# A decoder layer with fp32r matmuls: the memory plan is shifted by 32 bytes so that the matmul operands begin at multiples of 64

## The reference

```
h = rms_norm(x, g_mix_pre)
z = h @ w_in                                   # 1024 -> 2048
y_a = pool_mixer(z[..., :256], ...)            # trailing means of 2, 4, 8, 16 rows, a 64x64 map per head
y_b = conformer_conv(z[..., 256:768], ...)     # gate, 31-tap depthwise convolution, layer norm, silu
y_c = chunk_spatial_gating(z[..., 768:1280], ...)
y_d = short_gated_conv(z[..., 1280:], ...)     # 3 taps
o = concat([y_a, y_b, y_c, y_d]) @ w_out       # 1024 -> 1024
x = x + rms_norm(o, g_mix_post)
f = rms_norm(x, g_ffn_pre)
f = square(relu(f @ w_up)) @ w_down            # 1024 -> 4096 -> 1024
x = x + rms_norm(f, g_ffn_post)
```

## The kernel before

| tile | bytes | begins at | mod 64 |
|---|---|---|---|
| raw, w_hi, w_lo | 16,384 each | 16,512; 32,896; 49,280 | 0 |
| act_hi (line 136) | 17,408 | 77,152 | 32 |
| act_lo | 17,408 | 94,560 | 32 |
| warm; xms, xroot, xinv (lines 139 to 143) | 4; 16 each, so 32 each | 111,968; 112,000 to 112,095 | |
| p1: c_gate, h_raw, b_raw, c_short, ch_ext | | 112,608 and on | 32 |
| p1: a_ext, win, pool_d, gpre, sig, p_raw, g_ext, x0, conv, sqcv, v_raw, v_n and the rest | | 133,120 and on | 0 |
| p2: o_sb, mixc, x_in, g_mix, f_sb | | 112,608 and on | 32 |
| p2: u_hi, u_lo | 17,408 each | 169,952; 187,360 | 32 |

## Time and profile before

### The profile page before, as it was taken

The page is one execution under the profiler, slowest core; times in us unless marked ns, Lnnn a source line. Parts: engine busy times, 40 slices in busy tenths (PEclk is TensorE's granted clock), DMA queues, the critical chain, the costliest instruction groups (busy, mean ns, idle before and its releaser), DMA issues.

```text
span 2278.0 us, 33025 instructions
## 1 busy us (share of the span) xinstructions
PE 2169.0 (95%) x14425; PEld 1964.6 (86%) x14425; DVE 1083.2 (48%) x1400; ACT 755.1 (33%) x1157; POOL 115.7 (5%) x205
## 2 busy tenths in 40 slices
PE   6999999994999999999999999999999989999996
PEld 5887778784798898989899898989889989999995
DVE  3687786866523334553333346433334553324343
ACT  4423232234232223443322344332324442313141
POOL 2010111110000000000000000000000000000000
PEclk9999999996899999999999999999999999999998
DMA  7754555553132224444222244532223433222221
GB/s 245 270 203 166 206 168 204 195 182 111 58 112 93 93 93 130 139 149 138 93 93 93 93 130 161 170 95 93 93 93 114 140 124 120 86 75 93 75 75 61
DMA packets 186084, 291.88 MB, mean 128 GB/s; under 512 B 6127, under 2 KB 162452, under 8 KB 177732
## 3 DMA queue, kind: packets, MB, share of 16 engines
q1 hardware_dynamic: 160244, 167.76, 22.9%
q0 software_dynamic: 24656, 120.96, 15.1%
q10 hardware_dynamic: 1040, 1.05, 0.1%
HBM read 247.24 MB, written 42.80 MB: 127 GB/s over the span
## 4 chain that ended last, share of the span: by engine, by line
PE 68%; issue 19%; DVE 6%; ACT 4%; DMA 3%; POOL 0%; POOLq 0%; ACTq 0%; DVEq 0%
PE mm L1748 22%; PE mm L1749 22%; PE mm L1750 22%; ACT w_hi L666 2%; DVE w_lo L1111 2%; DMA mixc<-mixT_scratch 1%; DMA x_in<-in_x_prompt 1%; PE tr L1753 1%; DVE conv L1155 1%; DMA raw<-in_w_in 1%; PE tr L1977 0%; PE mm L1808 0%; DVE o_sb L1450 0%; PE tr L1774 0%; DVE conv_s L1659 0%
## 5 line engine op out<-in xcount | busy, mean ns | idle before, releaser
L1111 DVE TENSOR_TENSOR w_lo<-raw,w_hi 128x2048 fp32r<-128x2048 f32 x152 | 348.5, 2292 | 711.6 <-ACT w_hi L666 711.5
L1748 PE MATMUL mm<-act_hi,w_hi 128*128 128x512 f32 (+1 forms) x1728 | 641.4, 371 | 11.5 <-DVE act_lo L1468 6.2
L1749 PE MATMUL mm<-act_lo,w_hi 128*128 128x512 f32 (+1 forms) x1728 | 635.2, 368 | 0.0
L1750 PE MATMUL mm<-act_hi,w_lo 128*128 128x512 f32 (+1 forms) x1728 | 632.3, 366 | 0.0
L1748 PE MATMUL mm<-w_hi,u_hi 128*128 128x256 f32 (+1 forms) x2176 | 609.3, 280 | 0.8
L1750 PE MATMUL mm<-w_hi,u_lo 128*128 128x256 f32 (+1 forms) x2176 | 608.6, 280 | 0.0
L1749 PE MATMUL mm<-w_lo,u_hi 128*128 128x256 f32 (+1 forms) x2176 | 607.5, 279 | 0.0
L666 ACT ACTIVATE w_hi<-raw 128x2048 fp32r<-128x2048 f32 x152 | 291.0, 1915 | 594.7 <-PE mm L1750 589.0
L1748 PEld LDWEIGHTS mm<-w_hi,u_hi 128*128 128x128 f32 (+1 forms) x2176 | 399.5, 184 | 4.8 <-DVE u_lo L1484 3.0
L1750 PEld LDWEIGHTS mm<-w_hi,u_lo 128*128 128x128 f32 (+1 forms) x2176 | 399.6, 184 | 1.2
L1749 PEld LDWEIGHTS mm<-w_lo,u_hi 128*128 128x128 f32 (+1 forms) x2176 | 397.6, 183 | 1.6
(11 more groups left out here) (243 smaller groups left out, 1350.9 us busy)
## 6 DMA issues: line engine op xcount, KB each, us to landing
raw<-in_w_ffn_up SPq DMA_DIRECT2D x64, 1024.0 KB, 5.4
raw<-in_w_ffn_down SPq DMA_DIRECT2D x64, 1024.0 KB, 5.1
w_hi<-whi_scratch POOLq DMA_DIRECT2D x24, 1024.0 KB, 5.2
w_lo<-wlo_scratch POOLq DMA_DIRECT2D x24, 1024.0 KB, 8.0
raw<-in_w_out SPq DMA_DIRECT2D x16, 1024.0 KB, 5.2
whi_scratch<-w_hi POOLq DMA_DIRECT2D x8, 1024.0 KB, 8.3
wlo_scratch<-w_lo POOLq DMA_DIRECT2D x8, 1024.0 KB, 10.7
mixc<-mixT_scratch POOLq DMA_DIRECT2D x16, 512.0 KB, 5.9
```

The lines of the kernel that those rows point to most:

```text
L1111: DVE.tensor_tensor(w_lo[:, s, :, :], raw[:, s, :, :], w_hi[:, s, :, :].bitcast(fp32), ALU.subtract)\
L1748: PE.matmul(out, whi, xhi, start=(k == 0), stop=False)
L1749: PE.matmul(out, whi, xlo, start=False, stop=False)
L1750: return PE.matmul(out, wlo, xhi, start=False, stop=(k == K - 1))
```

## The change

`warm` is allocated before `act_hi` and no longer behind `act_lo`: `act_hi` and `act_lo` begin 32 bytes later, at 77,184 and 94,592. The three tiles `xms`, `xroot` and `xinv`, which took 96 bytes, become three parts of one tile `x_stats` of 48 bytes, rounded up to 64: every tile behind it, those of p1 and of p2 with `u_hi` and `u_lo` among them, begins 32 bytes earlier, `u_hi` at 169,920 and `u_lo` at 187,328. The four begin at multiples of 64. No instruction, wait or semaphore is added or removed, and all that uses the three names reads and writes the same elements as before.

```diff
         junk = sb("junk", [P, D], bf16)
         junk_o = sb("junk_o", [P, PC], bf16)
         junk_y = sb("junk_y", [P, PC], bf16)
+        warm = sb("warm", [P, 1])
+
 
         act_hi = sb("act_hi", [P, K, NX], f32r)
         act_lo = sb("act_lo", [P, K, NX], f32r)
 
-        warm = sb("warm", [P, 1])
-
-        xms = sb("xms", [P, NCH])
-        xroot = sb("xroot", [P, NCH])
-        xinv = sb("xinv", [P, NCH])
+
+        x_stats = sb("x_stats", [P, 3, NCH])
+        xms, xroot, xinv = (x_stats[:, i, :] for i in range(3))
         sms = sb("sms", [NS, 3])
         oms = sb("oms", [P, NCH + 1, NP])
         osum = sb("osum", [P, NCH + 1])
```

## The result

The changed kernel takes 2255.09 us (median of 4 runs, 2253.35 to 2255.92) against 2274.12 for the kernel before (its three runs and one more): ratio 0.9912, 95% interval 0.9897 to 0.9928. That is 19 us less, where 9 were forecast. The order of the work is the same; the busy line of the page answers to the earlier trace rows, with matmuls 28.8 and weight loads 22.3 us less busy and the other engines within 1.2 us of before.

What follows compares the result with a forecast made beforehand. The prediction took TensorE's matmul pitch as the bound; 9.3 us less from the moving operand, with all other terms zero, took the profiled 2279.85 us to 2270.6 and the median to 2265 us, with an 8-in-10 range of 2190 to 2290.

Steps and rivals of the forecast that it cites:

- What bounds the kernel: Whole kernel: TensorE's own pace, matmuls busy 2169.0 of 2278.0 us; memory places matter through matmul pitch or few waits.
- the small operations and transfers: ScalarE, VectorE, DMA, x_stats and warm: zero cost, with bounds of 2 ns an instruction and 0.5 us on few loads.
- The stationary operand: 8,736 matmuls of 256 columns, act or u stationary: zero effect taken, with 87 us of gain as one end.
- Both say zero, which I take: Stationary operand: transposes at 273 against 272 ns and 32-column loads with the 128-column pitch, read as zero effect.
- if D moves as much as U: Sign of a wrong mechanism: D stretches were to stay at 11.20 and 45.18 us while U stretches fell.
- The moving operand: 5,184 matmuls of 512 and 272 columns with act moving: 1.8 ns less each once aligned to 64, 9.3 us.
- The addresses: act and u start 32 bytes past multiples of 64, weights on multiples; the change puts all on multiples of 64.
- the likeliest case: Only the moving operand's alignment gains: 2265 us, own range 2255 to 2271, chance 0.35.
- Whole pieces: Rival: reader fetches 64-byte pieces, alignment saves one per matmul; 2237 us, or 2190 with the stationary operand; chance 0.22.
- No change: Rival: the excess has nothing to do with 64, the 1.8 ns being a curve in length; 2274 us, chance 0.22.
- Loads and stream meet: Rival: all 13,920 matmuls, weight loads and moving columns in one 64-byte phase collide; 25 us slower, 2299, chance 0.21.

Runs made afterwards that it cites:

- same-places run: Small tiles packed and unused pads added against the kernel before, act and u kept at 96 modulo 128 bytes; ratio 0.9998 (0.9989 to 1.0008).
- the last run: Against the kernel before, only the last block's U panels cut at column 256 instead of 272, act and u still at 96 modulo 128; 2279.62 us, one run.
- the exchange: Places swapped against the changed kernel: act at 64 and u at 0 modulo 128 bytes, instead of act 0 and u 64; 2271.81 us, one run.
- u alone: Against the kernel before, only u moved, to 64 modulo 128 bytes, act kept at 96; 2256.01 us, ratio 0.9928 (0.9904 to 0.9952).
- best plan: Against the kernel before, act and u both put at 64 modulo 128 bytes, weights at 0; 2241.61 us, ratio 0.9857 (0.9839 to 0.9874).

## Why the prediction was wrong

**What bounds the kernel: right.** The change acted through TensorE's pitch alone, the small operations and transfers cost nothing that shows, as priced (the sum of the matmul stretches leaves nothing for them; the same-places run had 0.9998), and the means of ScalarE's and VectorE's groups stayed within 4 ns where 2 were allowed (conv, the largest, 746 to 743).

**The stationary operand: the step that failed.** The prediction took zero from "Both say zero, which I take". D, where u is the stationary operand, brought 20.6 of the 22 us by the stretches, 18.6 by the sum over the traces. By the prediction's own sign it was wrong in mechanism "if D moves as much as U": four D panels moved by 1.21 us, four U panels by 0.23. The two rows that said zero could not say it. The transposes' 273 and 272 ns are durations, which the prediction itself had set aside as no pitch, and these matmuls run at half the column rate (their starts are 109 ns apart for 128 columns), where there is next to no excess to be removed. The 32-column loads were compared at distance 96 only, where the pitch is 117 for both lengths; at distance 0 they differ by 4 ns. A row that shows no difference at one place is no bound for another place.

**The moving operand: mis-sized.** 1.8 ns on 5,184 matmuls, 9.3 us. Measured: 1.2 ns on the 3,648 of 512 columns, 4.4 us, and nothing on the 1,536 of 272. The interpolated 118.5 ns for 256 columns off a multiple was itself good: in the trace of the last run the 256-column U matmuls at 96 are 118.6 ns apart on average. The error was to set it against D's 116.7 and call the difference alignment. The two rows differed also in which operand was moving, and both had an operand off.

**The addresses: too coarse.** The working noted the places modulo 64, as the change words it. Modulo 128 it would have seen that act goes to 0 and u to 64, and that O and D need not go one way.

**The number.** That 2255.09 us lies in the stated 2190 to 2290, and at the very edge of the 2255 to 2271 given to the likeliest case, is luck. That case had the gain in U and none in D.

**The rivals.** Whole pieces: fallen, since aligned O is slower and the exchange, aligned too, gave 2271.8. No change: right for 272 columns only. Loads and stream meet: the mechanism nearest to what the runs show, with both its sign and its place half right. It said that operands in one 64-byte phase would collide everywhere; they do at distance 0 (O, +2 ns against a forecast +1.6), and do the reverse at 64 (D, -3.4). Its evidence against, the pitch of the short loads, held only for the old distance.

**The pages.** The Trainium skill (SBUF — State Buffer, Specifications) names 16-byte lines, from which the second rival, no change, had starts 32 bytes apart alike. The runs do not agree that starts at multiples of 16 are alike: 32 bytes of u are worth 3.2 ns a matmul (96 to 64), and 16 bytes 4.1 (64 to 80). The Trainium skill (TensorE: Matmul & The Clock Gate, Step-by-step: what each phase is for) says that the weight load has a read port of its own and takes nothing from the running matmul. Here, with everything but the distance the same, D's pitch is 113.4 or 118.9 ns, and at distance 0 it is 118.9 behind a full load and 114.6 behind a small one. That does not agree, and the measurement decides; the ports themselves no row shows.

What stays open: how the memory is divided so that 64 bytes of 128 is the good distance; why 80 and 32 are both worse than 96; why at 96 D has two pitches modulo 256 and O has one; and why the 272-column matmuls, and U's 256 columns, gain so little. The runs show these and do not explain them. That the load of the next weights and the stream of the moving columns disturb each other is the reading that fits the distance and the short loads; the collision itself no row shows. Nor can the runs tell the load of a matmul's own weights from that of the next, since the high and the low tiles have the same place in every plan.

## What to carry to other kernels

For streams of fp32r matmuls with a weight load each, write down the places of both operands modulo 128 bytes and put the stationary and the moving one 64 apart; here that was 1.4% of the kernel for no instruction. Check it there by a run: it held for 256 columns in D and O and for 512 in U, and hardly for 272. Aligning a tile to 64 is not the point: it can help one stage and hurt the next, so read each stage's pitch from a stretch with a known count. And before a row is used as a bound of zero, ask whether the effect could have shown in it.

## What the runs showed of the hardware

- The pitch of a 256-column fp32r matmul behind a full weight load is 113.4 to 118.9 ns at the 2.4 GHz level, and goes with the distance of the operands' addresses modulo 128 (D stretches of 96: 10.88 us at 64, 11.20 at 96, 11.41 at 0). Columns alone are 106.7. For 512 columns it is 229.9 to 234.4, with 64 best here too, but 0 better than 96.
- Moving both weight tiles by 64 bytes gave the same three lengths, to 0.01 us, as moving act and u against them. The effect is one of relative address.
- It is sharp: from 64 to 80 the four-panel D stretch goes from 43.98 to 45.56 us.
- At distance 96 the address modulo 256 counts too. In D stretches of 96, matmuls are 118.6 ns apart where u is at 224 and w at 128 modulo 256, and 114.6 where u is at 96; with u moved by 128 the even and odd slices k change roles (114.7 and 118.5). At distance 64 (changed kernel, u alone, best plan) both are 113.3 to 113.6. In the O stretch of 96 at distance 96 even and odd k are alike, 116.7 and 116.8.
